# Query panels 2 to 7 as fp32 products on weights that ScalarE scales, row 0 chosen in one block, and another order of the first gathers

## The reference, cut to what matters

```python
def peer_ffn(z, peer_wq, keys1, keys2, peer_u, peer_v):      # z = rmsnorm(h, norm2_g)
    def chunk(zc):                                            # 128 tokens
        q = (zc @ peer_wq).reshape(128, 8, 2, 128)            # 8 heads, two halves
        s1 = einsum('chd,hkd->chk', q[:, :, 0], k1)           # 128 keys each
        s2 = einsum('chd,hkd->chk', q[:, :, 1], k2)
        v1, i1 = top_k(s1, 16); v2, i2 = top_k(s2, 16)
        cand = v1[..., :, None] + v2[..., None, :]            # 256 pairs
        top_s, top_pos = top_k(cand, 16)
        expert = take(i1 * 128 + i2, top_pos)
        gate = softmax(top_s)
        u = take(peer_u, expert)                              # rows of 2048 floats
        act = gelu(einsum('chkd,cd->chk', u, zc))
        v = take(peer_v, expert)
        return einsum('chk,chkd->cd', gate * act, v)
```

## Time and profile before

| | us |
|---|---|
| median of 3 runs | 2484.34 (2482.23 to 2484.65) |
| the profiled execution | 2483.83 |
| its span, first to last instruction | 2482.0 |
| busy: TensorE matmul / VectorE / ScalarE / GpSimd | 2133.8 / 1505.8 / 694.4 / 718.6 |
| mean granted TensorE clock, share of full | 0.953 |
| moved by DMA | 756.68 MB, of which 540.12 by the gathers' queue q0 |

### The profile page before, as it was taken

How to read it: one execution, slowest core, us unless ns; L and a number is a source line. 1 busy time by engine, 2 the same in 40 slices (tenths; PEclk the granted TensorE clock), 3 DMA queues, 4 the chain that set the end, 5 groups by cost and what they waited for, 6 DMA issues and landing times.

```text
span 2482.0 us, 32162 instructions
## 1 busy us (share of the span) xinstructions
PE 2133.8 (86%) x11988; PEld 1577.5 (64%) x11988; DVE 1505.8 (61%) x2166; ACT 694.4 (28%) x1159; POOL 718.6 (29%) x658
## 2 busy tenths in 40 slices
PE   7999999999999999999887767876687768776686
PEld 7999999999999999999833323332233223332232
DVE  5445665555646676767966555665555655655545
ACT  5435555544434445544211000100000000100001
POOL 3000000000002414121674444444344434444441
PEclk9999999999999999999898889988998889888998
DMA  9645454655666455565999999999999999999997
GB/s 275 212 144 154 152 154 151 193 180 179 216 213 205 152 164 170 167 206 196 404 422 421 421 422 422 421 422 422 421 422 422 422 421 422 422 421 422 422 422 298
DMA packets 281772, 756.68 MB, mean 305 GB/s; under 512 B 12160, under 2 KB 213328, under 8 KB 214992
## 3 DMA queue, kind: packets, MB, share of 16 engines
q0 software_dynamic: 74816, 540.12, 52.6%
q1 hardware_dynamic: 206624, 215.28, 27.8%
q10 hardware_dynamic: 240, 0.07, 0.0%
HBM read 752.26 MB, written 2.10 MB: 304 GB/s over the span
## 4 chain that ended last, share of the span: by engine, by line
PE 52%; DMA 35%; DVE 8%; issue 2%; POOL 2%; ACT 1%; ACTq 0%; DVEq 0%; POOLq 0%
PE PS L1769 40%; DMA RZ<-in_peer_u,idxu 18%; DMA RAW<-in_peer_u,idxu 16%; PE PS L2050 8%; DVE RZ L1615 2%; DVE RAW L1615 2%; DVE WL L1108 1%; POOL EX L637 1%; DMA EX<-in_peer_v,idxv 1%; PE PS L1899 1%; PE PS L1975 1%; DVE SM L1615 1%; PE PS L1875 0%; PE PS L1888 0%; PE PS L2014 0%
## 5 line engine op out<-in xcount | busy, mean ns | idle before, releaser
L2050 PE MATMUL PS<-EX,RK 128*128 128x512 f32 x1968 | 910.1, 617 | 312.7 <-ACT RK L1073 188.6
L2050 PEld LDWEIGHTS PS<-EX,RK 128*128 128x128 f32 x1968 | 378.5, 197 | 843.6 <-issue 710.8
L1769 PE MATMUL PS<-XH,WH 128*128 128x256 f32 x2832 | 782.8, 285 | 5.4 <-DVE SM L1203 2.4
L1769 PE MATMUL PS<-XH,WL 128*128 128x256 f32 x2832 | 776.9, 283 | 0.0
L1769 PE MATMUL PS<-XL,WH 128*128 128x256 f32 x2832 | 706.6, 283 | 0.0
L1108 DVE TENSOR_TENSOR WL<-RAW,WH 128x1024 fp32r<-128x1024 f32 x380 | 472.2, 1254 | 368.9 <-ACT WH L726 365.6
L1769 PEld LDWEIGHTS PS<-XH,WH 128*128 128x128 f32 x2832 | 544.4, 192 | 9.9 <-DVE WL L1108 5.4
L726 ACT ACTIVATE WH<-RAW 128x1024 fp32r<-128x1024 f32 x380 | 399.3, 1059 | 533.9 <-PE PS L1769 525.4
L1769 PEld LDWEIGHTS PS<-XH,WL 128*128 128x128 f32 x2832 | 544.5, 192 | 0.0
L1769 PEld LDWEIGHTS PS<-XL,WH 128*128 128x128 f32 x2832 | 502.3, 192 | 0.3
L1615 DVE CUSTOM_DVE_ANT_0 RZ<-RZ 128x2048 f32<-128x2048 f32 x126 | 288.8, 2292 | 249.2 <-DMA RZ<-in_peer_u,idxu 248.8
(11 more groups left out here) (339 smaller groups left out, 1273.4 us busy)
## 6 DMA issues: line engine op xcount, KB each, us to landing
RAW<-in_w_in SPq DMA_DIRECT2D x110, 1024.0 KB, 5.2
RAW<-in_w_out SPq DMA_DIRECT2D x32, 1024.0 KB, 5.6
RAW<-in_w_ple_gate SPq DMA_DIRECT2D x16, 1024.0 KB, 5.7
RAW<-in_peer_wq SPq DMA_DIRECT2D x16, 1024.0 KB, 6.3
RAW<-in_w_up_a SPq DMA_DIRECT2D x8, 1024.0 KB, 5.7
RAW<-in_w_up_b SPq DMA_DIRECT2D x8, 1024.0 KB, 5.7
EX<-in_peer_v,idxv POOLq DMA_INDIRECT x252, 26.5
RZ<-in_x SPq DMA_DIRECT2D x2, 1024.0 KB, 6.2
```

The costliest lines, as they stand in the source:

```text
L1769: ins = mm(o[:, t, :], left, right, start=(begins and k == t == m == 0), stop=(ends and k == QUARTER_KT - 1 and m == len(pairs) - 1), skip ...
L2050: ins = mm(bank(4 * (1 - hf) + c), left, right[:, 512 * c:512 * (c + 1)], start=False, stop=True, skip_group_check=True)
```

## The change

- Panels 0 and 1 stay as they are. For panels 2 to 7 ScalarE writes quarter by quarter weights times norm2_g (4 activations of 128x256 per quarter, one scale per partition) in fp32 to `scaled`, which lies on `WH`; TensorE multiplies these with h2 itself in plain fp32, 32 matmuls of 128x256 a panel (`whole_product`). VectorE does no splits for them. SyncE's loads from panel 4 on wait for `wh_ready` (ScalarE) instead of `wl_ready`.
- `WL`, `XH` and `XL` are free after product 1, so six V gathers of row 0 are issued between the U gathers of row 0; the V buffers are numbered anew. The U gathers of row 0 now go round four buffers outside `RAW`.
- VectorE chooses row 0 in one block behind query 0, makes `znat` afterwards, and then does the dots of row 0 with queries 2 to 5 and the pieces of row 1 at fixed dots between them.
- TensorE does `mean_square` ahead of the last quarter of product 0 and key scores 0 within the token order; key scores 1 to 6 stand ahead of the last quarter of the next product. ScalarE takes the root before its last split of panel 1.

The core of the diff (the rest is a semaphore, the copy of norm2_g and the removed tables of VectorE):

```diff
-        EARLY = [SM[:, 0:D], SM[:, D:2 * D], znat[:, 1, :], qhigh, SM[:, 0:D], SM[:, D:2 * D], znat[:, 1, :], qlow,
-                 raw_unit(6, 0), SM[:, 0:D], raw_unit(6, 1), SM[:, D:2 * D], znat[:, 1, :], raw_unit(7, 0), qlow, raw_unit(7, 1)]
-        EARLY_DOTS = {4: 1, 5: 2, 6: 3, 7: 4, 9: 5, 11: 6, 12: 7, 14: 8}
+        EARLY = [sm_a, sm_b, z_b, qhigh, sm_a, sm_b, z_b, qhigh, sm_a, sm_b, z_b, sm_a, sm_b, z_b, sm_a, sm_b]
+        EARLY_DOTS = {4: 1, 5: 2, 6: 3, 7: 4, 8: 5, 9: 6, 10: 7, 11: 9, 12: 10, 13: 11, 14: 12, 15: 13}
+        EARLY_VALUES = {3: 0, 5: 1, 7: 2, 9: 3, 11: 4, 13: 5}
+        scaled = view(EX, 0, QUARTERS, QUARTER_KT, PANEL)
...
-        vbuf = [view(EX, s * D, D) for s in (0, 2, 4, 6, 1, 3, 5, 7)]
+        vbuf = [view(EX, s * D, D) for s in (2, 3, 4, 5, 6, 7, 0, 1)]
...
+                if k in EARLY_VALUES:
+                    if EARLY_VALUES[k] == 0:
+                        g.wait_ge(S["w_used"], quarters_before("wq", SPLIT_Q))
+                    gather_v(0, 0, EARLY_VALUES[k], reused=False)
+            for k in range(4):
+                g.wait_ge(S["wh_ready"], quarters_before("wq", 6 + k // 2) + 2 * (k % 2) + 2)
+                gather_u(1, 1, k, reused=False)
+            g.wait_ge(S["w_used"], QUARTERS * PANELS)
+            for k in range(6, V_SLOTS):
                 gather_v(0, 0, k, reused=False)
+            g.wait_ge(S["h2t_done"], 2)
+            for k in range(4, U_AHEAD):
                 gather_u(1, 1, k, reused=False)
...
+            def scale_next(j, quarters):
+                n, before = STARTS["wq"] + j + 1, quarters_before("wq", j + 1)
+                for q in quarters:
+                    slot, at = 2 * (n % 2) + q // 2, QUARTER_KT * (q % 2)
+                    a.wait_ge(w_landed[slot], unit_landed("wq", j + 1))
+                    a.wait_ge(S["w_used"], before + (q + 1 - QUARTERS))
+                    for k in range(QUARTER_KT):
+                        m = QUARTER_KT * q + k
+                        ins = a.activation(scaled[:, q, k, :], raw[:, slot, at + k, :], ACT.Copy, scale=gain3[:, m:m + 1])
+                    ins.then_inc(S["wh_ready"], 1)
...
+            queries = {4: 2, 6: 3, 10: 4, 13: 5}
+            second = {4: (0, 1), 5: (2, 3), 6: (4, 5), 7: (6, 7), 8: (8, 9), 9: (10,)}
+            for k in range(TOPK):
+                if k in queries:
+                    query(queries[k])
+                dot(0, 0, 0, k, EARLY[k])
+                if k == 4:
+                    v.wait_ge(S["sc_evac"], 2)
+                for piece in second.get(k, ()):
+                    choose(1, 1, CHOOSE, piece)
...
+            query(6)
+            query(7)
+            def whole_product(j, third=None):
+                b = bank_of("wq", j)
+                pe.wait_ge(bank_free[b], evacuated("wq", j))
+                for q in range(QUARTERS):
+                    if q == 3 and third is not None:
+                        third()
+                    pe.wait_ge(S["wh_ready"], quarters_before("wq", j) + (q + 1))
+                    for k in range(QUARTER_KT):
+                        n = QUARTER_KT * q + k
+                        for t in range(2):
+                            ins = mm(tiles2(b)[:, t, :], scaled[:, q, k, t * P:(t + 1) * P], h2T[:, n, :],
+                                     start=(n == t == 0), stop=(n == KT - 1), skip_group_check=True)
+                    ins.then_inc(S["w_used"], 1)
```

More of the change, by code:

```diff
@@ L142 @@
 U_SLOTS, U_AHEAD = 8, 6
-SCORED = 4
+SPLIT_Q = 2
+SCORED = 7
 def build(nc, T, out):
@@ L418, in load @@
                     slot = 2 * (n % 2) + u
-                    if n >= 2:
+                    if section == "wq" and j >= SPLIT_Q + 2:
+                        sp.wait_ge(S["wh_ready"], quarters_before(section, j) + (2 * u + 2 - 2 * QUARTERS))
+                    elif n >= 2:
                         sp.wait_ge(S["wl_ready"], quarters_before(section, j, i) + (2 * u + 2 - 2 * QUARTERS))
@@ L1032, in key_scores @@
                              ACT.Copy).then_inc(S["sc_evac"], 1)
-            for j in range(8):
-                if j < 7:
-                    split_next("wq", j, quarters=(0, 1) if j == 1 else (0, 1, 2))
-                if 1 <= j <= SCORED:
+            def scale_next(j, quarters):
[8 more added lines that the diff above has]
+                    ins.then_inc(S["wh_ready"], 1)
+            a.wait_ge(S["gain_ready"], 1)
+            for j in range(8):
+                if j < SPLIT_Q - 1:
+                    split_next("wq", j, quarters=(0, 1, 2))
+                elif j < 7:
+                    scale_next(j, range(3))
+                if 2 <= j <= SCORED:
                     key_scores(j - 1)
-                if j < 7:
-                    split_next("wq", j, quarters=(2, 3) if j == 1 else (3,))
                 if j == 0:
@@ L1043, in _ @@
                     a.activation(rt[:], bank(3)[:, 0:TOK], ACT.Sqrt, scale=1.0 / D, bias=eps[:, 0:1]).then_inc(S["rt_ready"], 1)
+                if j < SPLIT_Q - 1:
+                    split_next("wq", j, quarters=(3,))
+                elif j < 7:
+                    scale_next(j, range(3, QUARTERS))
+                if j == 0:
+                    key_scores(0)
                     token_norm(0)
@@ L1633, in weights @@
                     .then_inc(S["w_ready"], 1)
[L1635 to L1673, removed]
@@ new lines, in query @@
+            def query(j):
+                b = bank_of("wq", j)
+                done("wq", j)
+                v.tensor_tensor(qp[:, 2 * j:2 * j + 2, :], tiles2(b), rstd2, ALU.mult).then_inc(bank_free[b], 1)
+            split_next("wq", 0, quarters=(0, 1, 2))
+            v.wait_ge(S["rt_ready"], 3)
+            do(v.reciprocal(rstd[:], rt[:]))
+            query(0)
+            split_next("wq", 0, quarters=(3,))
+            v.wait_ge(S["sc_evac"], 1)
+            for piece in range(11):
+                choose(0, 0, 0, piece)
@@ new lines, in _ @@
+            v.tensor_copy(idxu[:, 0, :], expf[:]).then_inc(S["idx_ready"], 1)
+            v.tensor_copy(idxv[:, 0, :], expf[:]).then_inc(S["idx_ready"], 1)
+            v.wait_ge(S["idx_ready"], 2)
+            query(1)
+            token_norm(0)
+            v.wait_ge(S["znat_ready"], 1)
+            queries = {4: 2, 6: 3, 10: 4, 13: 5}
[8 more added lines that the diff above has]
+                    choose(1, 1, CHOOSE, piece)
+                if k == 9:
+                    v.tensor_copy(idxu[:, 1, :], expf[:]).then_inc(S["idx_ready"], 1)
+                    v.wait_ge(S["idx_ready"], 3)
@@ L2007, in _, with token_order @@
                 ins.then_inc(S["keys_t"], 1)
-            def token_order(hf):
+            def token_order(hf, between=None):
                 b = 4 * (1 - hf)
                 for k in range(KT):
+                    if k == 6 and between is not None:
+                        between()
                     ins = mm(bank(b + k // 4)[:, (k % 4) * P:(k % 4 + 1) * P], h2T[:, k, hf * P:(hf + 1) * P], ident[:],
@@ L2031, in key_scores @@
                 ins.then_inc(S["sc_done"], 1)
[L2033 to L2040, removed]
+            def whole_product(j, third=None):
+                b = bank_of("wq", j)
+                pe.wait_ge(bank_free[b], evacuated("wq", j))
[9 more added lines that the diff above has]
+                    ins.then_inc(S["w_used"], 1)
+            product("wq", 0, operand="z3", third=lambda: mean_square(1, 1))
+            pe.wait_ge(S["keys_evac"], 4)
+            pe.wait_ge(S["h2_ready"], 8)
+            token_order(0, between=lambda: key_scores(0)).then_inc(S["h2t_done"], 1)
+            product("wq", 1)
+            for j in range(SPLIT_Q, 8):
+                whole_product(j, third=(lambda: key_scores(j - 1)) if j <= SCORED else None)
             for h in range(SCORED, PEER_HEADS):
```

22 lines of the change are left out of this document (4 added, 18 removed).

## The result

The changed kernel takes 2492.7 us (median of 6), the kernel before, timed beside it, 2483.7.

A forecast was written before the change was run, and what follows sets the result against it. Bytes through the DMA engines at 422 GB/s bound the kernel's end. Profiled 2483.8 - 1240.2 + 1242.4 (E, end of TensorE's last product) = 2486.0 us; range 2477 to 2494, the forecast's own 2480 to 2490.

The forecast's parts named there:

- The end is a sum of bytes: Gather rows run at 422 GB/s, so the end moves only by the DMA engines' idle time before that regime holds.
- The hole: DMA idle time near the last product's end, while value gathers wait behind it: E + 4 - 1236.1 us.
- E: The time at which TensorE ends the last of the query products, panels 2 to 7; forecast 1242.4 us.
- Start of the gathers: First gather of row 0 issued at 1148.0, 18.3 us earlier, flow full from 1151; 8.1 us won.
- The products: Panels 2 to 7 on TensorE take 13.8 us each, 14.7 with key scores, ending at 1234.9 if TensorE never waits.
- gain = 1240.2 - E: Start's 8.1 us less the later hole; each microsecond TensorE waits in panels 2 to 7 costs one at the end.
- How long TensorE waits: Weight units beside gathers take 14.2 or 11.0 us, so waits put E at 1243.7 or 1238, midway 1240.9 before the clock.
- the slower rival: Weights of panels 6 and 7 come last, TensorE stops twice for 5 us or more, clock falls; 2492.6 us, chance 0.30.
- the upper end: Top of the range, 2494 us, with E at 1250.6.
- the case with 0.05: Eight to one split of gather and weight bytes: a weight unit takes 23 us, E = 1253.2, 2496.8 us; chance 0.05.
- The clock: TensorE's granted clock may fall after a stop of 6 us, costing 1.5 us; 3.5 were lost in the kernel before.
- The rival that the change doesn't do what it says: Key scores 0 inside the token order hold up choosing row 0; 2493 us if query 0 is 5 us late; within slower case.

The follow-up runs named there:

- e4_vlate: The changed kernel with the six V gathers of row 0 issued after the sixteenth U gather instead of between the U gathers; 2476.5 us.
- e7_start: e4_vlate with the first gather waiting until product 2 has ended and VectorE's evictions of panels 2 to 5 earlier among the dots; 2485.6 us.
- e3_half: The changed kernel with half the matmuls of panels 2 to 7 left out; 2480.5 us.
- e2_two: The changed kernel with the second weight unit of each of panels 4 to 7 issued by ScalarE on its own DMA queue; 2491.0 us.
- e1_wide: The changed kernel with weight units of panels 4 to 7 read as 128 rows of 8 KB, from wrong places, instead of 1024 1 KB pieces; 2483.9 us.
- e6_2k: The changed kernel with weight units of panels 4 to 7 read in 512 pieces of 2 KB instead of 1024 of 1 KB, from wrong places; 2483.7 us.
- e8_vlate_wide: e4_vlate with e1_wide's 8 KB weight rows (wrong weights); 2476.4 us.

## Why the prediction was right and wrong

**The end is a sum of bytes: right.** In the table's profiled executions each MB that was not moved by 1265 us costs the same. Between the changed kernel and e4_vlate it is (2492.8 - 2476.5) / (46.1 - 39.5) = 2.5 us per MB; 422 GB/s are 2.4. A line through these two gives 2483 for the kernel before (profiled 2483.8), 2486 for e7_start (2486.2) and 2481 for e3_half (2480.7); the other four lie within 0.6 us of it, but e2_two is 1.2 above. The hole was forecast at E + 4 - 1236.1, 18.0 us for the measured E; the window from 1225 to 1265 has a share of 0.56, which is 17.6 us idle.

**Start of the gathers: right.** 1147.21 for a forecast of 1148.0, full flow in the window from 1150 (from 1151). Its price, 8.1 us, fits: the windows from 1150 to 1170 have no idle time left, and e7_start lost 9.1 us for 16.0 of the forecast's 18.3, of which 2.4 can be E's.

**The products: right.** Panels take 13.82 us (13.8), product 2 starts at 1146.08 (1146.7), and where nothing waits the last one ends at 1234.2 in e4_vlate (forecast for that case: 1234.9). ScalarE's scaling stayed hidden except where its weights were late.

**gain = 1240.2 - E: right.** For the changed kernel it gives -9.9 (measured -9.0), for e1_wide -1.8 (-0.6), for e4_vlate +6.0 (+6.8). It gives about 1 us too little each time. It holds while the start stays where it is; e7_start breaks it, since its start moved.

**How long TensorE waits: this step failed.** It took a unit of weights at 14.2 or 11.0 us beside gathers, and so E at 1242.4. The rows under it, 4.92 to 1.11 MB and 4.4 to one, mixed stretches in which the gather queue was full with stretches in which it was empty, for before the change the U gathers alone waited for their buffers. The change itself filled these pauses with V gathers. Read off where both queues are full, the unit is 21 us. The packet counts of the same rows tell it: 1106 of weights to 664 of gathers and 1223 to 544, where two full queues have 736 to 739. Neither unit time belonged to the new schedule: the prediction named the reason ("V rows fill the pauses now") and yet worked with the old mixture, at 14.2 us a unit at the most. The mechanism was the forecast's, the size was the slower rival's: E = 1249 and 2492.6 forecast there, 1250.1 and 2492.7 measured. Its picture of two stops in panels 6 and 7 was not met: TensorE stopped once for 12.5 us, in the middle of product 5, and once for 0.8. That the measured time lies inside the range at all is in part luck: the upper end was worked out from units of 14.2 us, a second stop and the full clock loss, and one long stop behind units of 21 us came to nearly the same sum.

The Trainium skill, DMA: Bandwidth & Descriptors, section Queues, rings and completion order, says that an engine serves its queues in turn, a packet of descriptors at a time. The prediction gave it 0.05, with a unit of 23 us, panel 5's second unit landing at 1205, product 6 at 1223.8 and E = 1253.2. The traces agree that the queues take turns of equal numbers of the trace's packets: 739 to 736 of 8 and 1 KB, 661 to 660 with 2 KB, 654, 654 and 653 with three queues. How many pass in one turn they do not show. That unit landed at 1208.9, product 6 began at 1220.4. So the case with 0.05 came within 3.1 us in E, and its time, 2496.8, stood outside the range. A ratio of bytes from a stretch where one queue is partly empty should have been no evidence against it.

**The clock.** Forecast at 1.5 us. In the stop of 12.5 us the granted clock fell to 0.50, the 1.2 GHz level, and over the 5 us behind it stood at 0.60, both levels mixed; the next quarter's 16 rows took 5.30 us, where 3.62 are usual behind a wait, 1.7 lost. After e1_wide's stop of 4.7 us it was 2.5. The 3.5 us that the prediction read off the kernel before hold 0.5 that is not clock: at full clock the same rows behind a wait take 1.17 and 3.84 us (e4_vlate). In e2_two 1.8 us were lost after a stop of 2.1 us (granted clock 0.66 from 1200 to 1205), in e6_2k 0.1 at the most after 3.2 and 2.6 (1.00): the length of the stop alone does not give the loss.

**The rival that the change doesn't do what it says** fell: the choosing ended at 1146.1, where 1146.8 was forecast.

What stays open: how much of the 9.1 us of e7_start is the start and how much the evictions that had to move with it, and whether the weights in 2 KB pieces with the right places (which needs two panels computed together) would allow V gathers to stay where the change put them. Neither was tried. Nor was it tried why two queues did worse than 2 KB pieces at the same rate of bytes.

## What to carry to other kernels

A share of the DMA engines read off a trace holds only for the queue fill at which it was read. Before a change fills the pauses of a queue, count packets per us where both queues are full, and set that beside what the consumer needs per us (here 49 against 139). An urgent stream of small packets beside a patient one of large packets is helped by larger pieces or by issuing the patient ones later, and less by a second queue that has two units travel at once; the cheapest cure here was an order of gathers, worth 16 us.

## What the runs showed that I had not expected

A second queue for the weights nearly doubled their packets (49 to 87 per us) and moved the median by 1.7 us, where 2 KB pieces at the same rate of bytes were worth 9. Speeding the weights up made the gathers late enough to stop TensorE at another place (a U row 19 us on its way in e1_wide). And by the profile's share 1 KB packets used the engines less well: in e4_vlate, 1190 to 1205, 2.58 MB of them took the same share as 3.18 MB of gathers,

```profile
q1 hardware_dynamic: 2554, 2.58, 52.6%
q0 software_dynamic: 436, 3.18, 52.6%
```

yet taking them away (e8_vlate_wide) changed nothing that could be measured.
